# Neighbourhood attention in tiles of 16 grid rows x 8 columns, differential attention on every eighth token

## What is computed

```python
h = rms_norm(x, mix_norm_w)                       # x (1024, 1024) and (256, 1024)
qa, ka, va, qd, kd, vd = split(h @ w_in, 6)       # 512 columns each

# neighbourhood attention: 8 heads of 64
row_start = clip(r - kh // 2, 0, rows - kh)       # kh = min(8, rows)
col_start = clip(c - 8, 0, 64 - 16)               # 16 columns wide
in_win = (c[None, :] >= col_start[:, None]) & (c[None, :] < col_start[:, None] + 16)
s = q . k over the 8 window rows, all 64 columns; * 1/8 + rpb[head, dr, dc]
s = where(in_win, s, -inf);  p = softmax(s);  o = p @ v;  ya = rms_norm(o, na_norm_w)

# differential attention: 4 heads, two halves of 64, v of 128, all keys of the group
bias = t5_table[t5_bucket(k_pos - q_pos)]
p = softmax(q . k / 8 + bias)                     # for each half
yb = rms_norm((p[0] - lam * p[1]) @ v, subln_w) * (1 - lambda_init)

x = x + concat(ya, yb) @ w_out
# 16 experts, each takes its best 2 n / 16 tokens of each group (expert choice)
x = x + moe(rms_norm(x, ffn_norm_w));  y = rms_norm(x, final_norm_w)
```

## Time and profile before

| | |
|---|---|
| median of 3 runs | 2779.84 us (2778.32 to 2779.93) |
| profiled execution | 2779.84 us, of which its span is 2778.1 us |
| PE busy | 2678.6 us (96%), 22988 matmuls |
| weight loads busy | 2521.4 us (91%) |
| DVE busy | 1978.8 us (71%) |
| ACT busy | 1715.2 us (62%) |
| POOL busy | 1096.0 us (39%) |
| DMA | 655.40 MB, mean 236 GB/s |

### The profile page before, as it was taken

The page is one execution under the profiler, slowest core; times in us unless marked ns, Lnnn a source line. Parts: engine busy times, 40 slices in busy tenths (PEclk is TensorE's granted clock), DMA queues, the critical chain, the costliest instruction groups (busy, mean ns, idle before and its releaser), DMA issues. The chain is left out here.

```text
span 2778.1 us, 54432 instructions
## 1 busy us (share of the span) xinstructions
PE 2678.6 (96%) x22988; PEld 2521.4 (91%) x22988; DVE 1978.8 (71%) x2350; ACT 1715.2 (62%) x2559; POOL 1096.0 (39%) x738
## 2 busy tenths in 40 slices
PE   7999999998986999999999999999999999999996
PEld 7877898877876999999999999999999999999996
DVE  5233326666467878878788787887878788787787
ACT  3366615555124676767667676676767767676675
POOL 2132220224112453636446263452735436364352
PEclk9999999999987999999999999999999999999998
DMA  7231110113354889889888898879888888898887
GB/s 190 52 101 40 48 55 30 40 56 104 139 225 163 311 277 332 285 316 318 289 308 285 318 315 309 314 260 335 300 308 313 286 321 285 318 315 289 321 284 282
DMA packets 357644, 655.40 MB, mean 236 GB/s; under 512 B 25752, under 2 KB 85016, under 8 KB 356888
## 3 DMA queue, kind: packets, MB, share of 16 engines
q1 hardware_dynamic: 341291, 606.41, 61.2%
q0 software_dynamic: 16112, 45.53, 6.1%
HBM read 616.48 MB, written 39.62 MB: 236 GB/s over the span
## 5 line engine op out<-in xcount | busy, mean ns | idle before, releaser
L1776 DVE TENSOR_TENSOR wl<-stg,wh 128x2048 bf16<-128x2048 f32 (+1 forms) x544 | 1243.9, 2292 | 276.5 <-ACT wh L1298 271.9
L1298 ACT ACTIVATE wh<-stg 128x2048 fp32r<-128x2048 f32 (+1 forms) x544 | 1010.9, 1861 | 203.4 <-PE S L944 78.9
L2120 POOL TENSOR_TENSOR hx<-hh,hx 128x320 fp32r<-128x320 f32 x176 | 384.8, 2186 | 814.7 <-ACT hx L1350 814.4
L941 PE MATMUL S<-X,wh 128*128 128x320 f32 x3760 | 591.9, 312 | 1.3 <-DVE X L1785 1.3
L941 PEld LDWEIGHTS S<-X,wh 128*128 128x128 f32 x3760 | 556.3, 188 | 3.9 <-issue 2.1
L987 PE MATMUL S<-hx,wh 128*128 128x320 f32 x1892 | 312.4, 313 | 4.9 <-DVE yTs L1824 4.9
L941 PE MATMUL OG<-X,wh 128*128 128x320 f32 x1872 | 298.4, 312 | 0.0
L944 PE MATMUL S<-Xb,wl 128*128 128x160 bf16 x3760 | 290.1, 233 | 0.0
L987 PEld LDWEIGHTS S<-hx,wh 128*128 128x128 f32 x1892 | 280.8, 188 | 6.8 <-issue 6.7
L941 PEld LDWEIGHTS OG<-X,wh 128*128 128x128 f32 x1872 | 277.2, 188 | 1.3 <-issue 1.1
L944 PEld LDWEIGHTS S<-Xb,wl 128*128 128x128 bf16 x3760 | 258.9, 98 | 12.0
(11 more groups left out here) (283 smaller groups left out, 4262.4 us busy)
## 6 DMA issues: line engine op xcount, KB each, us to landing
stg<-in_w_gate_dram SPq DMA_DIRECT2D x80, 2048.0 KB
stg<-in_w_up_dram SPq DMA_DIRECT2D x80, 2048.0 KB
stg<-in_w_down_dram SPq DMA_DIRECT2D x64, 2048.0 KB
stg<-in_w_down_dram SPq DMA_DIRECT2D x32, 1536.0 KB
stg<-in_w_gate_dram SPq DMA_DIRECT2D x16, 1024.0 KB
stg<-in_w_up_dram SPq DMA_DIRECT2D x16, 1024.0 KB
w_st<-in_w_in_dram SPq DMA_DIRECT2D x20, 512.0 KB, 3.8
yt<-mixed SPq DMA_DIRECT2D x10, 512.0 KB, 4.5
```

The source lines that it names most:

```text
L941: pe.matmul(out, w, x, start=first, stop=False, skip_group_check=True)
L1298: act.activation(piece_conv(wh, g), piece_stage(g), ACT.Copy).then_inc(rounded, 1)
L1776: dve.tensor_tensor(piece_conv(wl, g), piece_stage(g), piece_conv(wh, g).bitcast(F32), ALU.subtract).then_inc(split, 1)
L2120: pool.tensor_tensor(hx[:, f, CT:2 * CT], hh[:, :, :], hx[:, f, 0:CT].bitcast(F32), ALU.subtract).then_inc(hidden_ready, 1)
```

## The change

The prompt tile of the first half becomes an *octet*: 16 grid rows x 8 columns, so tile t is columns 8t to 8t + 7, and its window lies in the tiles t - 1, t and t + 1. `na_window` gives 384 keys (256 for the first and last tile and for the sample). x is loaded in that order (`in_octets`), and `hT_tile` puts column p of tile t at position 8p + t of `hT`: neighbouring columns of one tile are 8 elements (32 bytes) apart. Read from the front, `hT` then holds at n = 128c + 8r + g the token 8 (8r + g) + c, so a plain slice of 128 is "every eighth token": that is the tile of the differential attention. `qk_cut` and `qk_sums` store a neighbourhood Q or K chunk by octets again, reading PSUM in steps of 8 elements. The T5 bias of a differential tile is read from `BT` in steps of 8 elements; its table in HBM is laid out by `BTW + TPR` per query row. Q gets a second buffer (`q_buffer`), since one chunk now belongs to all octets. Ranks of chosen tokens follow the new order (`tri_eq`), tokens have new numbers in `NG`, and stores and loads of rows are by octets or by every eighth row. Sample tiles are as before, except that a separate small table (`TS`, `BS`) serves them.

```diff
+def na_window(t):
+    if t >= TPR:
+        return TPR, NSA
+    first, last = max(t - 1, 0), min(t + 1, TPR - 1)
+    return first, (last - first + 1) * P
...
+    def in_octets(rows, t):
+        return rows.rearrange("(r g c) d -> g c r d", r=GR, c=OC)[t]
...
+    def q_buffer(j):
+        return j % 2 if j < JOBS else 0
+
+    def hT_tile(buf, k, t):
+        if t < TPR:
+            return buf[:, k, t:NPR:TPR]
+        return buf[:, k, t * P:(t + 1) * P]
+
+    def qk_cut(buf, j, c):
+        _, t0, ln = CHUNK[c]
+        if j < JOBS and t0 < NPR:
+            return buf[:, 0:NPR].rearrange("p (g q) -> p g q", g=TPR)[:, :, t0 // TPR:(t0 + ln) // TPR]
+        return buf[:, t0:t0 + ln]
+
+    def qk_sums(j, c):
+        _, t0, ln = CHUNK[c]
+        out = OG[:, 1 if j else c % 2, 0:ln]
+        if j < JOBS and t0 < NPR:
+            return out.rearrange("p (q g) -> p g q", g=TPR)
+        return out
...
             def na_table(j):
                 for hh_ in range(2):
+                    q = (2 * j + hh_) * NDR
                     for up in range(2):
-                        q = (2 * j + hh_) * NDR
-                        src = G_d[:, q:q + NDR, GW - 1:2 * GW - 1]
-                        sp.dma_start(TE[j % 2][GW * up:GW * up + GW, hh_, up:up + NDR, :], src).then_inc(te_in[j % 2], 16)
+                        sp.dma_start(TS[j % 2][GW * up:GW * up + GW, hh_, :, :],
+                                     G_d[:, q + 5 - up:q + 11 - up, GW - 1:2 * GW - 1]).then_inc(te_in[j % 2], 16)
+                    for r in range(GR):
+                        r0 = row_start(r)
+                        d0 = q + r0 - r + NA_KH - 1
+                        sp.dma_start(TR[j % 2][r:P:GR, hh_, r0:r0 + NA_KH, :],
+                                     G_d[0:OC, d0:d0 + NA_KH, GW - 1 - OC:GW - 1 + 2 * OC]).then_inc(te_in[j % 2], 16)
...
+                def h_of(buf, k):
+                    return hT_tile(buf, k, t) if n < V_B else buf[:, k, tok]
                 for k in range(KT):
-                    mm = three(S[:, n // 2 % 2, n % 2 * 512:n % 2 * 512 + 256], hT_h[:, k, tok], hT_l[:, k, tok],
+                    mm = three(S[:, n // 2 % 2, n % 2 * 512:n % 2 * 512 + 256], h_of(hT_h, k), h_of(hT_l, k),
                                hi(k), lo(k), k == 0, k == KT - 1)
...
-                act.activation((Kh[j % 2] if i else Qh)[:, t0:t0 + ln], OG[:, 1 if j else c % 2, 0:ln], ACT.Copy,
+                act.activation(qk_cut(Kh[j % 2] if i else Qh[q_buffer(j)], j, c), qk_sums(j, c), ACT.Copy,
                                scale=(1.0 if i else SCALE)).then_inc(fill_hi, 1)
...
-                    bias_max(s, c, S[:, c, 0:nk], BT[h % 2][:, (TPR - 1) * P - tl * P:(TPR - 1) * P - tl * P + nk],
-                             E[:, 2 * (s % 2) + c, 0:nk])
+                    src, dst = S[:, c, 0:nk], E[:, 2 * (s % 2) + c, 0:nk]
+                    if t < TPR:
+                        tab = BT[h % 2][:, TPR - 1 - t:TPR - 1 - t + NPR].rearrange("p (q c) -> p c q", c=TPR)
+                        src, dst = (x.rearrange("p (c q) -> p c q", c=TPR) for x in (src, dst))
+                    else:
+                        tab = BS[h % 2][:, (1 - tl) * P:(1 - tl) * P + nk]
+                    bias_max(s, c, src, tab, dst)
...
+                if j < JOBS:
+                    for t in range(TPR):
+                        pool.dma_start(in_octets(cut[0:NPR, :], t), o_all[j % 2][:, t, :]).then_inc(done, 16)
```

More of the change, by code:

```diff
@@ L36 @@
 BIG = 3e38
+BT0 = TPR * (P - 1)
+BTW = 2 * NPR + P * TPR
 JOBS8 = 2 * JOBS
@@ L269, in build @@
     mask = after("mask", [P, GW], F32)
+    mask_lr = after("mask_lr", [P, 2, OC], F32)
+    col_of = after("col_of", [P, 1], F32)
+    from_col = after("from_col", [P, OC], F32)
     ssx = after("ssx", [P, 2 * TT], F32)
@@ L683, in scores @@
                 if s < NAS:
-                    kt0, nk, _, inner = na_window(t)
-                    k0, chunks = kt0 * P, [(0, 0, 288), (512, 288, 288)] if inner else [(0, 0, nk)]
+                    kt0, nk = na_window(t)
+                    k0, chunks = kt0 * P, [(0, 0, nk)]
                 else:
@@ L694, in scores @@
                             rows = slice(64 * hf, 64 * hf + 64)
-                            mm = pe.matmul(S[:, hf, at_:at_ + ln], a[rows, q], b[j % 2][rows, kk],
+                            mm = pe.matmul(S[:, hf, at_:at_ + ln], a[q_buffer(j)][rows, q], b[j % 2][rows, kk],
                                            start=(n == 0), stop=(n == 2))
@@ L705, in exp_blocks @@
                 nk = na_window(t)[1]
-                return [En[:, 2 * (s % 2) + hf, b * P:min(nk, (b + 1) * P)] for hf in range(2) for b in range(na_blocks(t))]
+                return [En[:, 2 * (s % 2) + hf, b * P:(b + 1) * P] for hf in range(2) for b in range(nk // P)]
             def turn_exps(s, fills):
@@ L1508, in na_bias @@
                 j, t = s // TT, s % TT
-                _, nk, row, inner = na_window(t)
+                nk = na_window(t)[1]
                 if t == 0:
@@ L1901, in _ @@
             own.wait()
+            own(pool.iota(msk_c[:, :], [[1, OC], [0, GR]], base=0, channel_multiplier=0,
+                          allow_small_or_imprecise_dtypes=True))
+            own.wait()
             pool.sem_inc(const_ready, 1)
@@ L1934, in bias_tables @@
             def bias_tables(j):
-                pool.wait_ge(te_in[j % 2], 64 * (j // 2 + 1))
+                pool.wait_ge(te_in[j % 2], 16 * 2 * (2 + GR) * (j // 2 + 1))
                 pool.wait_ge(mask_ready, 1)
-                te = TE[j % 2][:, :, :, :].rearrange("p h r c -> p (h r) c")
-                own(pool.tensor_tensor(te, te, mask[:, :].unsqueeze(1).to_broadcast([P, 32, GW]), ALU.add))
-                own.wait()
-                if j:
-                    pool.wait_ge(scores_read, 2 * ((j - 1) * TT + 6))
-                stand()
-                for h in range(2):
-                    own(pool.tensor_copy(TI[:, h, :], TE[j % 2][:, h, 3:12, :].rearrange("p r c -> p (r c)")))
-                own.wait()
-                stand()
-                own(pool.memset(TI[0:GW, :, 8 * GW:9 * GW], MASKED))
-                own(pool.memset(TI[GW:P, :, 0:GW], MASKED))
+                stand()
+                te = TS[j % 2][:, :, :, :].rearrange("p h r c -> p (h r) c")
+                own(pool.tensor_tensor(te, te, mask[:, :].unsqueeze(1).to_broadcast([P, 12, GW]), ALU.add))
+                for b, u, side in ((0, 0, None), (1, 0, 0), (2, 1, None), (3, 2, 1), (4, 2, None)):
+                    for h in range(2):
+                        out = TB[j % 2][:, b, h, :].rearrange("p (c r) -> p c r", c=OC)
+                        cols = TR[j % 2][:, h, :, OC * u:OC * u + OC].rearrange("p r c -> p c r")
+                        if side is None:
+                            own(pool.tensor_copy(out, cols))
+                        else:
+                            own(pool.tensor_tensor(out, cols, mask_lr[:, side, :].unsqueeze(2).to_broadcast([P, OC, GR]),
+                                                   ALU.add))
                 own.wait()
@@ L2013, in list_constants @@
                 own(pool.memset(one[:, :], 1.0))
+                own(pool.memset(tri_eq[:, :], 1.0))
                 own(pool.memset(posm[:, :, NE:NE + 2], 0.0))
@@ L2032, in list_constants @@
                 own(pool.memset(NG[:, :, NE:NE + 2, 2:PARTS], 0.0))
+                own.wait()
+                own(pool.affine_select(out=tri_eq[:, :], in_=tri_eq[:, :], compare_op=ALU.is_ge, fill=0.0, base=0,
+                                       pattern=[[1, P]], channel_multiplier=-1))
                 own.wait()
```

178 lines of the change are left out of this document (105 added, 73 removed).

## The result

The changed kernel takes **2840.56 us** (median of 4 runs, 2838.44 to 2842.68), the kernel before beside it 2779.89: ratio **1.0218**, 95% interval 1.0205 to 1.0231. The forecast was 2819, in a range of 2744 to 2880. It is slower, as forecast, by 60.7 us instead of 39. The profiled execution has a span of 2840.9 us, 62.8 more than before; the page shows where the busy time went.

A forecast was written before the change was run, and what follows sets the result against it. PE was taken to bound the neighbourhood jobs and V stage, with a ring about as fast as PE in jobs 4 to 6. Terms -34.4 + 34.9 + 6 + 31.6 + 1.5 = +39.6 on 2779.84: 2819 us, range 2744 to 2880.

The forecast's parts named there:

- Neighbourhood jobs, -34.4: Four neighbourhood jobs: fewer keys cut PE's scores, values and turns by 8.6 us a job, -34.4 us in all.
- V stage, +34.9: V passes for neighbourhood heads: 384 weight loads of 128 columns in steps, 0.71 ns an element, 91 ns each: +34.9 us.
- Rival 2: V stage: weight loads don't mind the step, DVE and ACT do; 2785 us, chance 0.16.
- Q and K chunks, +6: Jobs 1 to 3: 12 prompt chunks read from PSUM in steps, 0.5 us each after slack: +6 us.
- T5 bias, +31.6: Differential jobs: 64 bias passes 0.73 us longer; 20 us in jobs 4 to 6, 11.6 in job 7.
- the ring: Jobs 4 to 6: bias, exponential, mix, next bias, turning about as fast as PE; spare only DVE's 19.5 us waiting for PE.
- Ranks, +1.5: Router's ranks: 14 more matmuls at 0.1 us each, with PE waited for by DVE: +1.5 us.
- SP's queue, 0: Before the first job: 72 table transfers at 0.43 us an issue, 31 us, end at 109.5, covered: no cost.
- rival 4: SP's queue late: 72 table transfers at 1.15 us each bring weights some 40 us late; 2859 us, chance 0.05.
- the main case: Whole kernel: the forecast itself, 0.71 ns an element for steps, +39.6 us, 2819 us; chance 0.42.
- Rival 1: All stepped reads are free, leaving the neighbourhood gain and the ranks: 2747 us, chance 0.20.
- rival 3: Stepped reads cost the doubled price, 1.42 ns an element: +125.5 us, 2905 us, chance 0.17.

The follow-up runs named there:

- e3: The changed kernel with the load of job 1's Q weights issued between the tables of job 0 and job 1, not after both: 2832.79 us.
- e8: The changed kernel with the tiles of x loaded as 128 rows in order, not by octets, in the first stage only: 2837.05 us.
- e9: The kernel before with only the first-stage loads of the prompt's x tiles changed, to octets of 8 blocks of 16 rows: 2796.00 us.
- e6: The changed kernel with hT written and read contiguously, by tile, in both V passes: 2811.34 us.
- e5: The changed kernel with Q and K chunks read from PSUM and written contiguously, not in steps of 8: 2843.16 us.
- e2: The changed kernel with the T5 table read contiguously in all prompt bias passes: 2806.76 us.
- e4: The changed kernel with the second V pass reading hT in contiguous tiles of 128, first pass and writes unchanged: 2822.90 us.
- e7: The changed kernel rebuilt without any step: all prompt tiles octets, T5 table reordered in HBM, e3's load order: 2777.94 us, ratio 0.9993 to the kernel before.
- e11: e7 with octet tokens ordered row by row, and output projection, residual, FFN input and router's ranks in octet order too: 2762.47 us.

## Why the prediction was right, and where it was off

The direction and the mechanism held: a gain of some 8 us a neighbourhood job, more than eaten by operands in steps. The size did not: the loss was 62.8 us where the sum had 39.6. The terms were off by +14.8 (V stage), +8.7 (SP's queue), +4.1 (T5 bias), +2.0 (jobs) and -6 us (chunks, which cost nothing and so hid a part of the other errors). Term by term:

- **Neighbourhood jobs, -34.4.** Measured with e3's order: -7.9, -16.5, -7.9, together -32.4. Unit prices were exact; the missing 2 us I did not trace.
- **V stage, +34.9.** Measured +49.7. Two errors. The step costs 238 - 118 = 120 ns a load, 0.94 ns an element, not the 0.71 taken from POOL (another engine, and a table of bf16): 384 x 0.12 = 46. Of these 43.1 show (e8 against before). Of the other 3, 1.7 were covered in the first pass, by a wait of PE for `hT_l` of a sample tile that only the kernel before has; the rest I did not trace. And "rows of x move in the same pieces: nothing" was wrong. Alone the loads cost 16.6 us (e9); behind the slower PE of this kernel 6.6 (e8), and 43.1 + 6.6 = 49.7. Taking the writes of hT in steps at nothing was right for the time, though each got longer: ACT's from 597 to 1168 ns, DVE's from 683 to 1138; in e8 PE waits for neither. That e6 gave back 35.8, nearly my number, is an accident of these two: with the steps gone the loads become the bound. Rival 2, that weight loads don't mind, fell.
- **Q and K chunks, +6.** Nothing (e5): ACT reads a chunk from PSUM in steps of 32 bytes in 598 ns and DVE in 691, as without steps. I had carried an SBUF price over to PSUM.
- **T5 bias, +31.6.** Measured +22.4 in jobs 4 to 6 and about +13 in job 7 (e2 gives back 13.3). A pass takes 2.09 us, 0.85 ns an element more. That 48 x 0.873 - 19.5 is just 22.4 is an accident, for the slack was not where I had put it. Of the 19.5 us that DVE waited for PE only 6.5 were used up (9.2 to 3.8 for scores, 10.3 to 9.2 for projections). Another 10.6 came from the wait for the second exponential, which I had counted as part of the ring with nothing to give: it fell from 1.71 to 1.31 us in a prompt step. With a pass of 2.1 us the first exponential, 1.15 us on ACT, is done before the second pass ends, and the second exponential need no longer queue behind it. So three waits covered 17.1 us of the 39 that DVE's busy time rose, which leaves 22. My sum had taken off 15 (35 - 20); the rest of the error is the low price.
- **Ranks, +1.5.** Job 7 to the end is 1.1 us longer in e2 than before: about right.
- **SP's queue, 0.** Wrong: 8.7 us in job 0 (e3). An issue costs 0.61 us, not 0.43, so the 72 take 45 us where I had 31, and the cover of 3 us that I had left was gone. That is rival 4's mechanism at a small part of its size, and it occurred together with the main case, which I had not allowed for.
- **POOL's nine stores a job, 0.** Right in jobs 0 to 3.

Rival 1 (free steps) fell, rival 3 (1.42 ns) too. The test I had named, one price per element in the V stage and in the bias pass, came out at 0.94 and 0.85 ns: near each other, and both above the 0.71 that I used.

## What to carry to other kernels

Price a change of layout at every reader and writer, transfers included: for a transfer look at the number of outermost blocks as well as at the size of a piece. Keep the fastest-moving step of fp32 in SBUF at 2 elements or fewer, and turn a small table once rather than read a large one in steps on the engine that sets the pace. When a stage gets shorter, list what it had covered: here three gains (e4, e7, e11) came out smaller than expected because a queue, a load or a store lost its cover or came late. A wait inside a ring is not fixed either: ask what makes it as long as it is, and whether a slower neighbour shortens it.

## What I had not expected of the hardware

- fp32 in SBUF, step 2: full rate on PE's weight loads and on DVE. Step 4 already costs the full price: 233 ns a load against 120, 2.0 us a pass against 1.22; up to step 32 it does not grow.
- PSUM in steps of 8: no cost for ACT (598 ns a chunk) or DVE (691 ns). PE was not tried.
- Writes to SBUF in steps of 8 do cost: 512 elements of hT took ACT 1168 ns in place of 597, and DVE 1138 in place of 683.
- A 512 KB load in 8 blocks of 16 rows ran at 122 to 150 GB/s with a DMA share near 0.5; as 16 blocks of 8 rows at 190 GB/s and 0.85. At most 10 packets of 4 KB were in flight in the first case, 16 and more in the second, and between 10 and 20 us a packet took some 110 ns longer in both than one of adjacent rows (161 ns).
- A small table transfer of 64 pieces took 0.61 us to issue on SP, where a small transfer before took 0.43.
